# The front of a DeltaNet and Hyena trunk as one straight program, its operands kept on chip, and the gates' series moved into the projections

## The reference, cut to what matters

```python
mod_x = jax.nn.silu(c) @ w_mod[i] + b_mod[i]
mod_c = jax.nn.silu(c_ctx) @ w_mod[i] + b_mod[i]
hc = rmsnorm(ctx_s, norm_g[i]) * (1.0 + sc_c) + sh_c
pc = project(hc, w_in[i])
hx = rmsnorm(x, norm_g[i]) * (1.0 + sc_x) + sh_x
px = project(hx, w_in[i])
...
g = -jnp.exp(lp['dn_a_log'][d]) * jax.nn.softplus(a_raw + lp['dn_dt_bias'][d])
beta = jax.nn.sigmoid(b_raw)
...
gc = jnp.cumsum(gc, axis=-1)
```

## Time and profile before

| what | value |
|---|---|
| median of 3 runs | 5008.45 us (5001.71 to 5015.25) |
| profiled execution, its own time | 5007.58 us |
| span in its profile | 5005.9 us |
| TensorE busy | 4402.2 us (88%) |
| VectorE, ScalarE, GpSimd busy | 2488.4 (50%), 1257.0 (25%), 1790.0 us (36%) |
| mean granted TensorE clock | 0.96 |

### The profile page before, as it was taken

The page is one execution under the profiler, slowest core; times in us unless marked ns, Lnnn a source line. Parts: engine busy times, 40 slices in busy tenths (PEclk is TensorE's granted clock), DMA queues, the critical chain, the costliest instruction groups (busy, mean ns, idle before and its releaser), DMA issues. The chain is left out here.

```text
span 5005.9 us, 70855 instructions
## 1 busy us (share of the span) xinstructions
PE 4402.2 (88%) x28049; PEld 2776.9 (55%) x28049; DVE 2488.4 (50%) x3580; ACT 1257.0 (25%) x2669; POOL 1790.0 (36%) x1486
## 2 busy tenths in 40 slices
PE   6226999999999999999996999888888887599998
PEld 6203565444444554444445888756555565477775
DVE  0555557245244677889315666545555555122121
ACT  0100121111122221111113555455555552000000
POOL 0022222333323334423228999543333332111111
PEclk9977999999999999999998999999999998799999
DMA  2543232222324333332427777554545444532230
GB/s 110 173 165 133 76 97 83 84 84 80 114 87 147 94 105 98 110 106 88 135 76 205 220 217 219 171 196 156 189 161 187 161 172 153 219 112 90 94 108 26
DMA packets 468584, 663.02 MB, mean 132 GB/s; under 512 B 125882, under 2 KB 360818, under 8 KB 450356
## 3 DMA queue, kind: packets, MB, share of 16 engines
q1 hardware_dynamic: 423812, 541.11, 32.9%
q0 software_dynamic: 25360, 100.67, 6.5%
q10 hardware_dynamic: 19104, 16.96, 1.0%
HBM read 423.30 MB, written 235.34 MB: 132 GB/s over the span
## 5 line engine op out<-in xcount | busy, mean ns | idle before, releaser
L1263 PE MATMUL proj_b<-proj_S,proj_tw 128*128 128x512 f32 x1920 | 850.8, 595 | 0.0
L1263 PE MATMUL proj_b<-proj_A,proj_wt 128*128 128x512 f32 x1280 | 589.7, 605 | 47.6 <-issue 26.3
L1263 PEld LDWEIGHTS proj_b<-proj_S,proj_tw 128*128 128x128 f32 x1920 | 362.3, 191 | 433.3 <-issue 432.9
L1263 PEld LDWEIGHTS proj_b<-proj_A,proj_wt 128*128 128x128 f32 x1280 | 248.0, 195 | 361.0 <-issue 338.8
L743 POOL TENSOR_TENSOR proj_tw<-proj_wt 128x512 f32<-128x512 f32 x80 | 111.7, 1396 | 925.7 <-PE proj_b L1263 889.3
L1263 PE MATMUL proj_b<-proj_S,proj_wt 128*128 128x512 f32 x640 | 292.2, 600 | 0.0
L1263 PE MATMUL proj_b<-proj_A,proj_tw 128*128 128x512 f32 x640 | 288.1, 593 | 2.0 <-DVE proj_u L1029 2.0
L2543 PE MATMUL mrg_b<-mrg_za,mrg_w_a 128*128 128x256 f32 x1024 | 233.0, 381 | 27.0 <-DMA mrg_w_o<-in_w_out_dram 27.0
L2543 PE MATMUL mrg_b<-mrg_yb,mrg_w_b 128*128 128x256 f32 x1024 | 231.5, 379 | 0.0
L2556 PE MATMUL mrg_b<-mrg_w_o,mrg_mt 128*128 128x512 f32 x512 | 221.9, 594 | 6.6 <-POOL mrg_mt L2429 6.6
L2543 PEld LDWEIGHTS mrg_b<-mrg_za,mrg_w_a 128*128 128x128 f32 x1024 | 195.3, 191 | 56.4 <-issue 30.7
(11 more groups left out here) (289 smaller groups left out, 8216.7 us busy)
## 6 DMA issues: line engine op xcount, KB each, us to landing
proj_wt<-in_w_in_dram POOLq DMA_DIRECT2D x80, 1024.0 KB, 6.0
delta_nv<-scratch_NV SPq DMA_DIRECT2D x144, 256.0 KB, 3.9
delta_kq<-scratch_KQ SPq DMA_DIRECT2D x128, 256.0 KB, 4.1
scratch_bounce_f<-fft_first SPq DMA_DIRECT2D x32, 1024.0 KB, 3.8
fft_yf<-scratch_bounce_f SPq DMA_DIRECT2D x32, 1024.0 KB, 5.7
scratch_bounce_i<-fft_yi SPq DMA_DIRECT2D x32, 1024.0 KB, 4.5
fft_second<-scratch_bounce_i SPq DMA_DIRECT2D x32, 1024.0 KB, 7.0
scratch_hy<-proj_tok SPq DMA_DIRECT2D x48, 512.0 KB, 2.6
```

The costliest lines, as they stand in the source:

```text
L1263: last = pe.matmul(bank[:, :], weights[:, k, :], aa[operand][:, k, :], start=(k == 0), stop=(k == KH - 1))
```

## The change

`modulate` and `gates` become one function, and every loop in it is written out. `w_mod` comes in 12 pieces of 1 MB (16 column products each), three deep; tokens five deep. TensorE alternates the transposes of the first 10 token tiles (256 context tokens and the first half) with the first 8 pieces, which hold scale and shift; the last 4 pieces (the output gate) follow the last 8 tiles. Tiles are first copied unscaled into `hT` by ScalarE (four blocks) and VectorE (four blocks); then `shape` applies scale and shift to whole windows, directly into the operand tiles `aa` and `hc`, which `project` shares. Only the second half's seven operands go through `comb`. Gate products put `k % 4` in strips of 32 partitions; a product with `sel` turns tokens to partitions and adds the four strips. The raw gates `z` (128 x 18 x 32) pass to `project`, where bias, series, decays and betas run on VectorE in the slots of steps 13 to 17, on 576 elements for each partition; sums and rows are made by TensorE in steps 15 and 16. `low` shares the memory of `x2`, so `gcT` and `low` are loaded at the end of step 52, and the second half's `zb` loads wait for the last piece's set-up.

```diff
-    "hT": (P, KT, TOK), "comb": (2, 7, P, KT // 2, SEQ // 4),
-    "sc": (P, NCH, H, 2, NQ),
+    "comb": (7, P, KT // 2, SEQ // 4),
     "KQ": (NCH, P, H, 2, CH), "NV": (NCH, P, H, 2, CH),
-    "gcT": (2, NCH, H, CH), "btT": (2, NCH, H, CH), "btK": (2, NCH, H, CH),
+    "gcT": (2, NCH, H, CH), "btK": (2, NCH, H, CH),
...
+        wm = kit.sb("wm", P, 3, KT, PIECE_COLS)
+        NX = 5
+        WINDOWS = [(0, CTX)] + [(CTX + QT * w, QT) for w in range(4)]
+        HEAD = 3
...
+        def part(w, k):
+
+            first, width = WINDOWS[w]
+            if w == 0:
+                return hc[:, k, :]
+            if w == 1:
+                return (aa["A11"] if k < KH else aa["A12"])[:, k % KH, :]
+            if w == 2 and k >= KH:
+                return aa["A22"][:, k - KH, :]
+            return hT[:, k, first:first + width]
+
...
+                wv = T["w_mod"][0].rearrange("(k p) n -> p k n", p=P)
+                for j in range(NPIECES):
+                    if j >= 3:
+                        sp.wait_ge(products, j - 2)
+                    sp.dma_start(wm[:, j % 3, :, :], wv[:, :, j * PIECE_COLS:(j + 1) * PIECE_COLS]).then_inc(w_in[j % 3], 16)
+                shaped_by_both(sp, 4)
+                for x in ("A11", "A12", "A22"):
+                    sp.dma_start(T["comb"][OPERANDS.index(x)], NEXT[x]).then_inc(S["comb_out"], 16)
...
+                for i in range(NCH):
+                    wait(pool, scaled, i - NX + 1)
+                    if i == HEAD_TILES:
+                        pool.wait_ge(products, 6)
+                    pool.dma_start(xin[:, i % NX, :], source(i)).then_inc(x_in[i % NX], 16)
+                shaped_by_both(pool, 2)
+                pool.tensor_tensor(aa["S3"][:, :, :], aa["A11"][:, :, :], quarter(2, 0), ALU.subtract).then_inc(differed, 1)
+                shaped_by_both(pool, 4)
+                pool.wait_ge(summed, 3)
+                pool.wait_ge(z_done, 3)
+                pool.wait_ge(differed, 1)
+                pool.tensor_tensor(NEXT["S3"], NEXT["A11"], NEXT["A21"], ALU.subtract).then_inc(differed, 1)
...
+                def square(i):
+                    act.wait_ge(x_in[i % NX], 16 * (i // NX + 1))
+                    wait(act, squared, i)
+                    act.activation(sq[:, :], xin[:, i % NX, :], ACT.Square, accum_out=ss[:, i:i + 1]).then_inc(squared, 1)
+                def root(i):
+                    act.wait_ge(meaned, i + 1)
+                    act.activation(sd[:, i:i + 1], ms[:, i:i + 1], ACT.Sqrt).then_inc(rooted, 1)
+                def move(i):
+                    act.wait_ge(turned, i + 1)
+                    act.activation(hT[:, KH:KT, i * P:(i + 1) * P], tile_banks(i)[1][:, :].rearrange("p (k t) -> p k t", t=P), ACT.Copy).then_inc(moved["act"], 1)
+                def tiles(first, last):
+                    for i in range(first, last + 2):
+                        if i < last:
+                            square(i)
+                        if first <= i - 1 < last:
+                            root(i - 1)
+                        if first <= i - 2 < last:
+                            move(i - 2)
+                def shape(w):
+                    a = 1 if w == 0 else 0
+                    first, width = WINDOWS[w]
+                    act.wait_ge(modulated, 2)
+                    for n in ("act", "dve"):
+                        act.wait_ge(moved[n], (first + width) // P)
+                    for k in range(KH, KT):
+                        last = act.activation(part(w, k), hT[:, k, first:first + width], ACT.Identity, scale=gsc[:, k, a:a + 1], bias=mod[:, k, a:a + 1])
+                    last.then_inc(shaped["act"], 1)
...
+                tiles(0, HEAD_TILES)
+                for w in range(HEAD):
+                    shape(w)
+                for w in range(2):
+                    keep(w)
+                tiles(HEAD_TILES, NCH)
+                for w in range(HEAD, 5):
+                    shape(w)
+                for w in range(2, 5):
+                    keep(w)
...
+                def mean(i):
+                    dve.wait_ge(squared, i + 1)
+                    dve.tensor_scalar(ms[:, i:i + 1], ss[:, i:i + 1], 1.0 / D, EPS, ALU.mult, ALU.add).then_inc(meaned, 1)
+                def scale(i):
+                    dve.wait_ge(rooted, i + 1)
+                    dve.reciprocal(rs[:, i:i + 1], sd[:, i:i + 1]).then_inc(inverted, 1)
+                    dve.wait_ge(inverted, i + 1)
+                    wait(dve, turned, i - 1)
+                    dve.tensor_scalar(xs[:, i % 2, :], xin[:, i % NX, :], rs[:, i:i + 1], None, ALU.mult).then_inc(scaled, 1)
+                def move(i):
+                    dve.wait_ge(turned, i + 1)
+                    dve.tensor_copy(hT[:, 0:KH, i * P:(i + 1) * P], tile_banks(i)[0][:, :].rearrange("p (k t) -> p k t", t=P)).then_inc(moved["dve"], 1)
...
+                def sums(n):
+                    if n == 1:
+                        for who in ("act", "dve"):
+                            dve.wait_ge(shaped[who], 3)
+                        dve.tensor_tensor(aa["S1"][:, :, :], quarter(2, 0), aa["A22"][:, :, :], ALU.add).then_inc(summed, 1)
...
+                def piece(j):
+                    pe.wait_ge(w_in[j % 3], 16 * (j // 3 + 1))
+                    for m in range(2 * j, 2 * j + 2):
+                        bank, col = (pm, 2 * m) if m < 2 * KT else (pg, 2 * (m - 2 * KT))
+                        for k in range(KT):
+                            last = pe.matmul(bank[:, col:col + 2], wm[:, j % 3, k, (m % 2) * P:(m % 2 + 1) * P], scond[:, k, :], start=(k == 0), stop=(k == KT - 1))
+                    last.then_inc(products, 1)
+                def tile(i):
+                    pe.wait_ge(scaled, i + 1)
+                    for n in ("act", "dve"):
+                        wait(pe, moved[n], i - 1)
                     for k in range(KT):
+                        last = pe.transpose(tile_banks(i)[k // KH][:, (k % KH) * P:(k % KH + 1) * P], xs[:, i % 2, k * P:(k + 1) * P], ident[:, :])
+                    last.then_inc(turned, 1)
+                def gate_products(w):
+                    first, width = WINDOWS[w]
+                    shaped_by_both(pe, w)
+                    wait(pe, z_out, w - 1)
+                    if w == 0:
+                        pe.wait_ge(gates_in, 16)
                     for k in range(KT):
+                        last = pe.matmul(pz[w % 2][RG * (k % 4):RG * (k % 4 + 1), 0:width], wbg[:, k, :], part(w, k), start=(k < 4), stop=(k >= 4))
+                    last.then_inc(z_done, 1)
+                def gate_turns(w):
+                    first, width = WINDOWS[w]
+                    pe.wait_ge(z_out, w + 1)
+                    if w == 0:
+                        pe.wait_ge(picked, 3)
+                    for c in range(first // P, (first + width) // P):
+                        last = pe.matmul(zt[c // 9][:, (c % 9) * RG:(c % 9 + 1) * RG], zs[:, w % 2, c * P - first:(c + 1) * P - first], sel[:, :], start=True, stop=True)
+                    last.then_inc(z_turned, 1)
+                for i in range(HEAD_TILES):
+                    tile(i)
+                    if 1 <= i < HEAD_TILES - 1:
+                        piece(i - 1)
+                gate_products(0)
+                gate_products(1)
+                for i in range(HEAD_TILES, NCH):
+                    tile(i)
+                gate_products(2)
+                for j in range(2 * KT // 2, NPIECES):
+                    piece(j)
+                for n in ("act", "dve"):
+                    pe.wait_ge(moved[n], NCH)
+                gate_turns(0)
+                gate_turns(1)
+                gate_turns(2)
+                for w in range(3, 5):
+                    gate_products(w)
+                for w in range(3, 5):
+                    gate_turns(w)
...
-                for x in OPERANDS:
-                    sp.dma_start(aa[x][:, :, :], T["comb"][0, OPERANDS.index(x)]).then_inc(a_in[0][x], 16)
-                sp.dma_start(hc[:, :, :], T["hT"][:, :, 0:CTX]).then_inc(hc_in, 16)
-                sp.dma_start(sc[:, :, :, :, :], T["sc"]).then_inc(sc_in, 16)
+                for row, name in ((dtb, "dn_dt_bias"), (alog, "dn_a_log")):
+                    sp.dma_start(row[:, :], T[name][0].rearrange("d h -> (d h)").unsqueeze(0).broadcast_to([P, 2 * H])).then_inc(terms_in, 16)
                 flat = lambda ap: ap.rearrange("c h t -> (c h t)").rearrange("(p n i) -> p n i", p=P // 2, i=SB)
                 halves = [slice(d * (P // 2), (d + 1) * (P // 2)) for d in range(2)]
-                for d in range(2):
-                    sp.dma_start(gcv[halves[d], :, :], flat(T["gcT"][d])).then_inc(gc_in, 16)
-                sp.dma_start(low[:, :], T["low"].broadcast_to([P, SB * SB])).then_inc(gc_in, 16)
...
+                        sp.wait_ge(istep, 2 * (4 + 2 * (SB - 2)) + 4)
                     sp.wait_ge(tok_out[m], 16 * tok_dmas[s - KT // 2 + 1])
...
+                        sp.wait_ge(g_out, 16)
```

(66 more changed lines are left out.)

511 lines of the change are left out of this document (215 added, 296 removed).

## The result

The changed kernel takes **4772.8 us** (median of 4 runs, 4770.5 to 4776.5), beside 5009.6 us for the kernel before on the same chip (4 runs): a ratio of 0.9531, 95% interval 0.9520 to 0.9542. The forecast was 4773.

What follows compares the result with a forecast made beforehand. The front was taken as a chain of waits, the projections as a TensorE stream: 5007.6 - 224.3 (front) - 12.9 (projections' start) + 2 (gate terms) = 4772.4; the median, 0.9 higher, is 4773 us, range 4724 to 4812.

Steps and rivals of the forecast that it cites:

- Small loads: Start of the front: small vectors, loaded beside bulk pieces and tokens, take 19 us, between bounds of 9.7 and 27.
- To the first transpose: Front, after the small loads: table loads, squares, scale, root and hops take 7 us, so TensorE starts at 26 us.
- Head: Front: ten token tiles and 8 of the 12 `w_mod` pieces on TensorE take 73.7 us, ending at 100 us.
- Gate products 0 and 1: Front, after the head: the first two windows of gate products take 2.6 and 4.3 us, done by 111 us.
- Rival C: Gate products: strips don't overlap, four or five windows at 6.9 us or more, +18 to +30 us, 4797 us; chance 0.12.
- Eight tiles: Front: the eight later token tiles, period 2.7 us, with sums delaying VectorE by 5 us, take 30 us, to 141 us.
- The rest of TensorE's front: From 141 us: gate products 2, four pieces, turns, gate products 3 and 4, end of block 1 at 186.5 us.
- Start of the projections: Block end to step 0's middle products: 15.8 us instead of 27.0, `proj_wt` loading almost alone; with 1.7 more, -12.9 us.
- Gate terms in the steps: Projection steps 13 to 17: 29 us of VectorE gate work in idle slots costs +2 us, bounds +1 and +30.
- rival D: Steps 13 to 17: gates overrun their slots and stall TensorE; all 29 us exposed give 4800, likely half; chance 0.13.
- Rival B: Front: the mixed stream of pieces, transposes and gate products takes the good pace, 46 us less, 4727 us; chance 0.12.
- Rival E: Projections: reads of operands at other addresses slow down, no gain; decided at 0.495 us an instruction instead of 0.443; chance 0.02.

Runs made afterwards that it cites:

- again: The changed kernel run once more without any edit, on a second chip: 4775.2 us, ratio 0.9534 to the kernel before.
- one_strip: The changed kernel with all eight products of a gate window on the same 32 partitions instead of four strips: 4787.8 us, ratio 0.9559.
- operands_reloaded: The changed kernel with the first half's seven operands also stored in device memory and loaded again at the start of the projections: 4795.5 us, ratio 0.9575.
- gates_at_once: The changed kernel with gate series, terms, decays and betas all in slot 0 of step 14 instead of eight slots: 4791.4 us, ratio 0.9565.

## Why the forecast held, point by point

1. **Small loads**, 19 us forecast, 22.3 measured. The bounds of 9.7 and 27 were right, and the reason too: with the bulk loads held back `sig` runs at 10.1 us, beside them at 22.3. (5.5 MB at 370 GB/s are 15 us and not 14; the 19 us were a middle of the bounds.)
2. **To the first transpose**, 7 us forecast, 5.1 measured: 27.5 against 26.
3. **Head**, 73.7 us forecast, 67.9 measured (27.47 to 95.4). The slow pace of 6.84 us was right for seven of the eight pieces; the first one took 3.92 us in this execution and 6.83 in `again`. Tiles took 1.74 of pitch. 95.4 against 100.
4. **Gate products 0 and 1**, 2.6 and 4.3 forecast, 1.94 and 3.64 measured, both at the lower level (granted 0.50). The 4.3 us had no working of their own: the forecast's prices for a full window were 2.6 and 5.3. Rival C is excluded by `one_strip`, and the strips overlap by 3.8 and not 2.7. "TensorEngine Tiling (Array Packing)" of the Trainium skill, overview, has up to four times; the trace agrees.
5. **Eight tiles**, 30 us forecast, 28.0 measured (105.2 to 133.26). The three sums weren't 2.2 us each: two were 2.28 and one was 6.58 beside GpSimd. I had put GpSimd's two subtractions under the pieces; the first of them isn't there.
6. **The rest of TensorE's front**, 45.5 us forecast, 37.1 measured (133.26 to 170.4): gate products 1.9 (4.3 forecast), four pieces 23.2 (25.9), ten turns 4.4 (3), the last two windows 5.7 (7), the last turns 2.0 (5.3 with copies and the end of the block). TensorE was thus done 16 us before the block end of the forecast. The step that failed is the sentence on the `comb` stores, "start near 147 us and end near 167, under the pieces": they ended at 181.8, because the S operands stand behind `gate_made` in SyncE's queue. The two errors nearly cancelled: block end 181.8 against 186.5. Reading SyncE's queue order in the diff would have shown it.
7. **Start of the projections**: 17.0 us against 15.8 forecast, and the 1.7 us of the products behind it came. 11.8 us saved against 12.9. The load was as forecast (the first product 6.6 us after the block's end, 7.0 forecast); the first two products and the turns of the convolution weights took 10.5 us instead of 8.8, the first of them 6.64 instead of 5.2. `operands_reloaded` shows the cause: the competing 7 MB.
8. **Gate terms in the steps**: +2 us forecast. From the middle products to the last one it is +1.8 us, and since 1.7 of step 0 are saved in it, the cost elsewhere is 3.5 us. In `again` it is +4.5, so one execution doesn't give this term to better than 3 us. TensorE is busy in 117.00 of 117 us of steps 13 to 17, so rival D is excluded. What remains, as far as the waits show it, is the sum products and turns on TensorE's path and 3.4 us of waits for `u3`, 2.0 before. `gates_at_once` gives the price of a wrong placement, 15 us.
9. **Later stages**, forecast untouched: +2.7 us in this pair of executions. In `again` it was 2372.5 (4775.0 - 2402.5), as before; so it is spread and not cost.

Rival B (the mixed stream takes the good pace) failed: the granted clock is 0.55 in the head, and the last four pieces begin at the upper level and are at 0.50 after 5 us, with TensorE never idle (the windows 135.10 to 140.10 and 140.10 to 145.10):

```profile
135.10:140.10 5.00, 5.00 (x47) 4.98 (x43) 3.07 (x7) 4.51 (x7) 0.42 (x1) 0.96 0.02 3
140.10:145.10 5.00, 5.00 (x25) 5.00 (x25) 4.96 (x2) 0.00 (x0) 5.00 (x1) 0.50 0.98 322
```

By part 1 of the Trainium skill's "TensorE: Matmul & The Clock Gate", as cited in the prediction, sustained activity would have held it; the trace is against this for column products. Rival E didn't occur: an instruction of the page group takes 849.7/1920 = 0.443 us. That the sum (-235.2 forecast, -234.6 measured) hit so closely is luck in part: TensorE was done with the front 16.1 us before the forecast end, and the stores gave 11.4 of them back. Term by term the misses are -4.7 (front), +2.8 (start), -0.2 (steps) and +2.7 us (later stages), +0.6 in all.

## What to carry to other kernels

When a front becomes one program, its end can be set by the last queue that drains and not by the busiest engine, as here by SyncE's: read the order of stores in the issuing queue, put the operands that the next stage waits for ahead of anything that waits on late work, and let vectors that are loaded value by value land before bulk loads start. Narrow products (two streamed columns) pay twice, in their fixed cost and in the level of TensorE's clock; make the wide matrix the streamed side and use strips. Work moved into an engine's gaps costs little as long as each part fits its slot (here some 3.5 us for 27 us of VectorE's work), and the price of one that doesn't is the gap plus the slower instructions behind it.

## What the runs showed of the hardware

- TensorE's clock: without idle time from 38 to 95 us, a stream of two-column products and transposes was granted 0.50. Two-column products alone, begun at the upper level, were at 0.50 after 5 us. With four 512-column products in each piece a head that had the upper level's pace ahead of the first of them kept it; with two a head that had the lower level's at that point never gained the upper, and the last pieces, begun at the upper level, lost it after some 3 and 6 us.
- The column of the granted clock can mislead. In the head with two fillers a piece it reads 1.00, as it does in the 82.1 us of the earlier trace rows, while a filler takes 2.06 us and not 1.10. The pace of a known instruction is the surer reading.
- A TENSOR_TENSOR on two on-chip operands of VectorE and one of GpSimd exclude each other, and the one that started first runs undisturbed: VectorE's took 6.58 instead of 2.28 us behind GpSimd's, GpSimd's 6.63 instead of 4.52 behind VectorE's.
- A store of 4 KB in single elements took 10.7 us to land with bulk stores behind it, with 81 GB/s for all of them together, and 11.6 us when it stood behind them; the same bulk stores ahead of it got 353 GB/s.
- Four strips of 32 partitions overlap by 3.8 for 512-column instructions at the upper level of the clock.
